# Two blocks of a small model on one core: the modulation vector computed beside three other stages, out of the first feed-forward

## What is computed

```python
c_act = jax.nn.silu(c)                       # c: (1, 1024)
ada = c_act @ w_ada[l] + b_ada[l]            # w_ada: (1024, 6144)
sh_m, sc_m, g_m, sh_f, sc_f, g_f = jnp.split(ada, 6, axis=-1)
h = modulate(rms_norm(x), sh_m, sc_m)        # h * (1 + scale) + shift
...                                          # second mixer: projections of h, rwkv and S5, w_out
x = x + g_m[:, None, :] * mix
h = modulate(rms_norm(x), sh_f, sc_f)
ffn = (jax.nn.silu(h @ ffn_w_gate[l]) * (h @ ffn_w_up[l])) @ ffn_w_down[l]
x = x + g_f[:, None, :] * ffn
```

## Time and profile before

| | us |
|---|---|
| median of 3 runs | 3499.85 |
| lowest and highest | 3493.99, 3503.96 |
| time of the profiled execution | 3495.26 |
| its span, first to last instruction | 3493.4 |
| PE busy | 3265.6 (93%) |
| DVE busy | 2001.5 (57%) |
| ACT busy | 1230.2 (35%) |
| POOL busy | 899.0 (26%) |
| granted clock of TensorE, mean | 0.957 of full |

### The profile page before, as it was taken

One profiled execution on the slowest core, in us unless ns is written; L12 is line 12 of the kernel. 1 busy time (PEld: TensorE's weight loads), 2 busy tenths in 40 slices (PEclk: granted clock), 3 DMA queues, 4 the chain that ended last, 5 costly groups with the idle time before them and its releaser, 6 DMA issues. The chain is left out here.

```text
span 3493.4 us, 56038 instructions
## 1 busy us (share of the span) xinstructions
PE 3265.6 (93%) x22553; PEld 2699.0 (77%) x22553; DVE 2001.5 (57%) x3144; ACT 1230.2 (35%) x2077; POOL 899.0 (26%) x502
## 2 busy tenths in 40 slices
PE   8999999999999989899899899979988979999999
PEld 7878888877887767777778777768776758888887
DVE  5852566533875567778778536144433355455685
ACT  3111222122665134344345421235332143333443
POOL 2332333346110432222200044132221332222000
PEclk9999999999999989999999999979998989999999
DMA  4454334334001423444374355220010313323742
GB/s 127 139 186 128 121 109 121 112 112 135 9 9 52 139 71 129 141 160 151 118 263 141 100 166 130 91 97 22 21 39 17 118 55 115 111 91 100 264 134 97
DMA packets 355294, 387.95 MB, mean 111 GB/s; under 512 B 27328, under 2 KB 258290, under 8 KB 353834
## 3 DMA queue, kind: packets, MB, share of 16 engines
q1 hardware_dynamic: 327518, 303.89, 28.2%
q10 hardware_dynamic: 26560, 78.27, 5.9%
q0 software_dynamic: 960, 2.21, 0.3%
HBM read 271.98 MB, written 112.33 MB: 110 GB/s over the span
## 5 line engine op out<-in xcount | busy, mean ns | idle before, releaser
L1104 PE MATMUL bk<-ffn_bhi,ffn_ahi 128*128 128x512 f32 x1240 | 492.2, 401 | 68.7 <-ACT ffn_u L1314 33.6
L1104 PE MATMUL bk<-ffn_blo,ffn_ahi 128*128 128x512 f32 x1240 | 487.8, 398 | 0.0
L1104 PE MATMUL bk<-ffn_bhi,ffn_alo 128*128 128x512 f32 x1240 | 486.9, 397 | 0.0
L1070 POOL TENSOR_TENSOR ffn_alo<-ffn_raw,ffn_ahi 128x512 fp32r<-128x512 f32 x134 | 222.8, 1673 | 722.1 <-ACT ffn_ahi L1245 722.1
L223 PE MATMUL acc<-h_hi,whi 128*128 128x512 f32 x1136 | 374.8, 409 | 23.2 <-DVE h_lo L2800 6.7
L223 PE MATMUL acc<-h_lo,whi 128*128 128x512 f32 x1136 | 358.1, 394 | 0.0
L223 PE MATMUL acc<-h_hi,wlo 128*128 128x512 f32 x1136 | 356.9, 393 | 0.0
L206 POOL TENSOR_TENSOR whi<-raw,ones 128x1024 fp32r<-128x1024 f32 (+1 forms) x83 | 155.9, 1879 | 755.7 <-PE acc L223 562.2
L1104 PEld LDWEIGHTS bk<-ffn_bhi,ffn_ahi 128*128 128x128 f32 x1240 | 238.9, 193 | 130.6 <-issue 77.0
L1104 PEld LDWEIGHTS bk<-ffn_bhi,ffn_alo 128*128 128x128 f32 x1240 | 239.1, 193 | 51.5
L1104 PEld LDWEIGHTS bk<-ffn_blo,ffn_ahi 128*128 128x128 f32 x1240 | 239.5, 193 | 49.9
(11 more groups left out here) (601 smaller groups left out, 6479.9 us busy)
## 6 DMA issues: line engine op xcount, KB each, us to landing
ffn_graw<-ffn_gated SPq DMA_DIRECT2D x154, 256.0 KB, 2.7
raw<-w_in SPq DMA_DIRECT2D x51, 512.0 KB, 4.0
projT<-proj_stage ACTq DMA_DIRECT2D x51, 512.0 KB, 3.1
ffn_ada_raw<-w_ada SPq DMA_DIRECT2D x12, 2048.0 KB, 8.9
ffn_raw<-w_up SPq DMA_DIRECT2D x44, 512.0 KB, 6.7
ffn_gated<-ffn_gout SPq DMA_DIRECT2D x44, 512.0 KB, 3.3
ffn_gated<-ffn_gt SPq DMA_DIRECT2D x22, 768.0 KB, 6.2
ffn_drow<-w_down SPq DMA_DIRECT2D x44, 256.0 KB, 6.0
```

Of the source, the lines that this page charges most:

```text
L1070: nc.gpsimd.tensor_tensor(a_lo[:, slot], source, a_hi[:, slot], ALU.subtract).then_inc(s[f"low{slot}"], 1)
L1104: ins = nc.tensor.matmul(o, wt[:, w, k, :], xt[:, x, k, :], start=first and i == 0, stop=last and i == 2, skip_group_check=reopened)
```

## The change

The modulation leaves the first feed-forward and becomes a class `Modulation`, used in three stages: 6 chunks beside the product with `w_out` in the first mixer output, 2 beside units 4 and 6 of the second projections, 4 beside units 2 to 5 of the second mixer output. The scaling on ACT and the tree on DVE become one chain on DVE: one `tensor_scalar` of 128x512 and seven `scalar_tensor_tensor` of 128x512, each of which waits for the one before it (`Steps.link`). The column sums stay on PE, the bias on DVE, which now adds the 1 of the scales too. A stage has one or two buffers of 2 MB for the matrix (`raw_at`); with `n` of them, load i waits on SP for the weighing of chunk i-n. `silu(c)` is computed in place by ACT at the start of the first mixer output. The second mixer's output is written out as a stage of its own, `second_mixer_out`, with the same order of work as `residual_gemm`.

```diff
@@ TwoNorms.programs
-            act.wait_ge(s["ada_ready"], 2)
...
-            for group in (1, 4):
-                c = prm[:, ADA + group * KD:ADA + (group + 1) * KD]
-                nc.vector.tensor_scalar(c, c, 1.0, None, ALU.add).then_inc(s["ada_ready"], 1)
@@
+class Modulation:
+    def load(self, sp, s, i):
+        n, c = len(self.raw), self.first + i
+        if i >= n:
+            sp.wait_ge(s["ada_part"], i - n + 1)
+        sp.dma_start(self.raw[i % n][:], self.w_ada[:, :, c * ADA_W:(c + 1) * ADA_W]).then_inc(s[f"ada_in{i % n}"], 16)
+
+    def weigh(self, dve, s, i):
...
+        dve.wait_ge(s[f"ada_in{i % n}"], 16 * (i // n + 1))
+        if i >= 2:
+            dve.wait_ge(s["ada_summed"], i - 1)
+        steps = Steps(dve, s["ada_step"], (KD - 1) * i)
+        steps.link(nc.vector.tensor_scalar(part[:], raw[:, 0, :], factor(0), None, ALU.mult))
+        for k in range(1, KD):
+            last = nc.vector.scalar_tensor_tensor(out=part[:], in0=raw[:, k, :], scalar=factor(k), in1=part[:], op0=ALU.mult, op1=ALU.add)
+            if k < KD - 1:
+                steps.link(last)
+        last.then_inc(s["ada_part"], 1)
+
+    def column_sums(self, pe, s, i, bank):
+        pe.wait_ge(s["ada_part"], i + 1)
+        if i > 0:
+            pe.wait_ge(s["ada_taken"], i)
+        for j in range(ADA_W // P):
+            last = self.nc.tensor.matmul(bank[:, j:j + 1], self.part[i % 2][:, j * P:(j + 1) * P], self.ones[:, 0:1], start=True, stop=True)
+        last.then_inc(s["ada_summed"], 1)
@@ attention_and_mixer_out: SP, PE, ACT, DVE
+                if u == KD + 1:
+                    sp.wait_ge(s["products_done1"], KD // 2)
+                if 0 <= u - KD - 1 < mod.count:
+                    mod.load(sp, s, u - KD - 1)
...
                 three_pass(nc, acc[b], w_hi[b], w_lo[b], x_hi, x_lo, n, ready=ready).then_inc(s[f"products_done{b}"], 1)
+                if 0 <= u - KD - 1 < mod.count:
+                    mod.column_sums(pe, s, u - KD - 1, ada)
...
+            c = prm[:, PRM["c_2"]:PRM["c_2"] + KD]
+            nc.scalar.activation(c, c, ACT.Silu).then_inc(s["c_done"], 1)
...
             for u in range(KD):
                 add(u)
                 add_square(u)
+                if 0 <= u - 2 < mod.count:
+                    mod.take(dve, s, u - 2, ada)
+                if u < mod.count:
+                    mod.weigh(dve, s, u)
@@ feed_forward: load_modulation, scale_modulation, weigh, column_sums, take and their calls go
@@ second_mixer_out (FIRST_CHUNK = 2): SP, PE, DVE
+                sp.dma_start(raw[b][:], weight(u)).then_inc(s[f"weight_loaded{b}"], 16)
+                if 0 <= u - FIRST_CHUNK - 1 < mod.count:
+                    mod.load(sp, s, u - FIRST_CHUNK - 1)
...
+                three_pass(nc, acc[b], w_hi[b], w_lo[b], hi, lo, KD, ready=ready).then_inc(s[f"products_done{b}"], 1)
+                if 0 <= u - FIRST_CHUNK - 1 < mod.count:
+                    mod.column_sums(pe, s, u - FIRST_CHUNK - 1, ada)
...
+                add(u)
+                add_square(u)
+                if 0 <= u - FIRST_CHUNK - 2 < mod.count:
+                    mod.take(dve, s, u - FIRST_CHUNK - 2, ada)
+                if 0 <= u - FIRST_CHUNK < mod.count:
+                    mod.weigh(dve, s, u - FIRST_CHUNK)
@@ projections2_and_s5: SP (behind the weights of unit u), PE, DVE (behind the read of unit u-1)
+                if u in (2, 4):
+                    mod.load(sp, s, u // 2 - 1)
...
                 if gh == 0:
+                    pe.wait_ge(s["ada_taken"], mod.count)
...
+                if u in (4, 6):
+                    mod.column_sums(pe, s, u // 2 - 2, tot[:, 0, :])
...
-            steps.do(nc.vector.memset(V[:, :, :, 0:1], 0.0))
...
+                if u in (5, 7):
+                    mod.take(dve, s, (u - 5) // 2, tot[:, 0, :])
+                if u in (4, 6):
+                    mod.weigh(dve, s, u // 2 - 2)
+                if u == Z_SLOT:
+                    dve.wait_ge(s["ada_summed"], mod.count)
+                    steps.do(nc.vector.memset(V[:, :, :, 0:1], 0.0))
@@ build: chunks (first, count) and the addresses in KB of the buffers for the matrix
+                            Modulation(nc, mem, env, "mix", w_ada, 0, 6, (40, 72), 100))
+    ... Modulation(nc, mem, env, "proj2", w_ada, 6, 2, (136,), 152) ...
+                     Modulation(nc, mem, env, "mix2", w_ada, 8, 4, (156, 172), 188))
```

More of the change, by code:

```diff
@@ L660, in _ @@
             sp.wait_ge(s["stored"], 16 * NT)
[L663 to L707, removed]
 def columns(w, k_tiles):
@@ L713, in columns, with __init__, take @@
     return lambda u: v[:, :, bass.ds(u * P, P)]
-def attention_and_mixer_out(nc, mem, env, projT, yaT, w_nsa, w_out, merged, sums, xmid):
-    xT, hi, lo = env["xT"], env["hi"], env["lo"]
+ADA_W = 4 * P
+class Modulation:
+    SEMS = "ada_in0 ada_in1 ada_step ada_part ada_summed ada_taken "
+    def __init__(self, nc, mem, env, name, w_ada, first, count, raw_at, part_at):
+        self.nc, self.prm, self.ones, self.w_ada, self.first, self.count = nc, env["prm"], env["ones"], w_ada, first, count
+        self.raw = [mem.at(f"{name}_ada_raw{i}", a, [P, KD, ADA_W]) for i, a in enumerate(raw_at)]
+        self.part = [mem.at(f"{name}_ada_part{i}", part_at + 2 * i, [P, ADA_W]) for i in range(2)]
+    def load(self, sp, s, i):
[4 more added lines that the diff above has]
+    def weigh(self, dve, s, i):
+        nc, n = self.nc, len(self.raw)
+        raw, part = self.raw[i % n], self.part[i % 2]
+        factor = lambda k: self.prm[:, PRM["c_2"] + k:PRM["c_2"] + k + 1]
+        dve.wait_ge(s[f"ada_in{i % n}"], 16 * (i // n + 1))
[15 more added lines that the diff above has]
+        last.then_inc(s["ada_summed"], 1)
+    def take(self, dve, s, i, bank):
+        n, c = ADA_W // P, self.first + i
+        out, bias = (self.prm[:, a + n * c:a + n * c + n] for a in (ADA, PRM["b_ada_2"]))
+        dve.wait_ge(s["ada_summed"], i + 1)
+        self.nc.vector.scalar_tensor_tensor(out=out, in0=bank[:, 0:n], scalar=1.0 if n * c // KD in (1, 4) else 0.0, in1=bias,
+                                            op0=ALU.add, op1=ALU.add).then_inc(s["ada_taken"], 1)
@@ L727, in attention_and_mixer_out @@
+def attention_and_mixer_out(nc, mem, env, projT, yaT, w_nsa, w_out, merged, sums, xmid, mod):
+    xT, prm, hi, lo = env["xT"], env["prm"], env["hi"], env["lo"]
     m_hi, m_lo = merged
@@ L738, in attention_and_mixer_out @@
     names = both("weight_loaded weight_high weight_split products_done acc_read other_in")
-    names += "gate_in0 gate_in1 gate_in2 gate_in3 gate_on summed high low square_done sum_done x_kept "
-    with phase(nc, mem, names, [(f"acc{b}", [P, NH, HALF], F32) for b in range(2)]) as (block, s, ps):
-        acc = [ps["acc0"], ps["acc1"]]
+    names += "gate_in0 gate_in1 gate_in2 gate_in3 gate_on summed high low square_done sum_done x_kept c_done " + mod.SEMS
+    banks = [(f"acc{b}", [P, NH, HALF], F32) for b in range(2)] + [("ada", [P, HALF], F32)]
+    with phase(nc, mem, names, banks) as (block, s, ps):
+        acc, ada = [ps["acc0"], ps["acc1"]], ps["ada"]
         def loads_of(u):
@@ L886, in half_rows, with feed_forward @@
     return order
-def feed_forward(nc, mem, env, name, up, down, kind, norm, sums, spill, xsave, gate=None, w_ada=None):
+def feed_forward(nc, mem, env, name, up, down, kind, norm, sums, spill, xsave, gate=None):
     xT, prm, ident, ones = env["xT"], env["prm"], env["ident"], env["ones"]
@@ L1176, in p3 @@
                 product(S4_B22, bank_c(p), False)
[L1178 to L1186, removed]
             def down_product(i, n):
@@ L1290, in high_s4 @@
                 high(S4_B22, s4[:], p + 1)
[L1292 to L1297, removed]
-                    nc.scalar.activation(ada_raw[:, k, :], ada_raw[:, k, :], ACT.Copy, scale=c_act[:, k:k + 1]).then_inc(s["ada_scaled"], 1)
             def high_t(slot, t, made):
@@ L1393, in _ @@
             high_t(A22_T4, T4, "t4_made")
-            if w_ada is not None:
-                nc.scalar.activation(c_act[:], prm[:, PRM["c_2"]:PRM["c_2"] + KD], ACT.Silu).then_inc(s["c_done"], 1)
             high_12(2)
@@ L1701, in _ @@
                     low_s3(p + 1)
-                if p in ada_chunks:
-                    weigh(ada_chunks[p])
             read_c12(LAST)
```

130 lines of the change are left out of this document (74 added, 56 removed).

## The result

| | before | changed |
|---|---|---|
| median of 6 runs, us | 3500.67 | 3520.91 |
| lowest and highest | 3493.99, 3506.26 | 3514.47, 3530.73 |
| ratio, 95% interval | | 1.0071 (1.0056 to 1.0085) |
| span of the profiled execution | 3493.4 | 3529.0 |
| PE busy | 3265.6 | 3279.5 |

The forecast was 3463, faster with a chance of 0.90. The change is slower by 20 us. The profiled execution of the changed kernel is its slowest (3530.73), that of the kernel before one of its shortest (3495.26), so the two profiles lie 35 us apart where the medians lie 20. So its stages are read one by one and its total is not used; to which stages the other 15 us belong, no trace shows.

A forecast was written before the change was run, and what follows sets the result against it. PE, busy 93% of the span, was taken as the bound. Terms -66.6 + 6.9 + 16.5 + 6 = -37.2 gave 3458 against the profiled execution, 3463 us with the median's 4.6; range 3447 to 3484.

The forecast's parts named there:

- The chain has a deadline, since PE makes chunk i's sums behind the next unit's products: First mixer output: PE waits 0.3 us for the first chunk's chain, 0.1 to 0.2 for each later one.
- The first feed-forward: Its up part loses waits on `copy_u2` and `copy_u3`, slow clock and column sums: -66.6 us.
- Its term for the clock: First feed-forward's up part: clock 0.97 against 1.00 over 446.2 us, worth 13.4 us.
- The chain: DVE's weighing of one chunk, one `tensor_scalar` and seven linked `scalar_tensor_tensor`: 6.0 us.
- the mixers' other terms: Column sums, chain waits and tail in the mixer outputs: +6.9 us in the first, +6 in the second.
- the half chance of POOL: Second mixer output: with half a chance, POOL once gets in before DVE's last link, 1.90 us more.
- The silu: Start of first mixer output: small activation and second table load end before the gate's landing; cost 0.
- The second projections: Unit 5's weights queue behind load 1, so PE idles, then half clock and sums: +16.5 us (13 to 21).
- the landing of the weights: Second projections: unit 5's weights land 8.5 to 9.5 us behind the large load's issue, later with other traffic.
- (a): Mixer outputs: POOL gets ahead of every chain's last link, 19 us, 25 with half clock: 3488; chance 0.11.
- (c): Second projections: stall lasts longer, units 6, 7 and S5's inputs late too, 26 for 16.5: 3473; chance 0.12.
- (d): First feed-forward's waits belong to convolution and GELU; only column sums come back, -10.8 against 29.4: 3518; chance 0.04.

The follow-up runs named there:

- experiment 8: Kernel before the change, once without two of the three tree additions: 3446.63 us; once without ACT's 96 scalings: 3476.91 us.
- the kernel of both: Changed kernel with two PSUM banks for the column sums and the second projections' second load moved behind unit 6's weights: 3445.70 us.
- experiments 3 and 4: Changed kernel with the second projections' second load behind unit 6's weights: 3513.39 us; the same with two PSUM banks for the column sums: 3445.70 us.

## Why the prediction was wrong

**The step that failed** is "The chain has a deadline, since PE makes chunk i's sums behind the next unit's products". It costed one of the two waits ahead of the sums, that for the chain, with care (0.3, then 0.1 to 0.2 each). The other, for the taking of the chunk before, appears in my text only as a small addition to the chain's length, "with the bias ahead of it 11.9". I asked how long the taking lasts and never where it stands. The earlier trace rows had the answer: the taking follows the addition that ends at 1191.22 + 2.83 = 1194.05, and PE reaches the sums just ahead of 1188.5, so 5.6 us of waiting for each chunk but the first of a stage. Eight times 5.6 is 45; measured 43.2 (the last of each stage waits 4.2, since no split runs beside it). With the 1.7 us of half clock that the text took for a short stall, the eight would have added 8 x 7.3 = 58 to -37: +21. That this is the distance of the medians, +20.2, is in part chance. By the stages of the two profiles the eight waits cost 43.2 + 26.4 = 69.6, with twice the clock of that sum, and the stages add up to +33.3. All the rest of the forecast, -37.2, came to 33.3 - 69.6 = -36.3, because its misses cancel: -0.6 in the feed-forward, -2.9 in the mixers, +4.4 in the projections.

**Point by point.** The first feed-forward: forecast -66.6, measured -67.2, waits on `copy_u2` gone, clock 1.00. The size is right; the cause is right but for the tree's own wait for ACT and for the sums, of which the text says nothing (experiment 8). Its term for the clock, 13.4, was 16.3 by PE's busy time (405.96 - 378.82 - 10.8), and leaves nothing for small gaps; the whole difference was taken, so the sum does not change. The chain: forecast 6.0, measured 0.47 + 7 x 0.75 + gaps, 1184.0 to 1190.0. The first chunk's wait: forecast 0.3, measured

```profile
1190.05 1.05 PE L708 MATMUL ada<-ones,mix_ada_part 128*128 128x1 f32 x8 [0.15 <-DVE mix_ada_part L698]
```

With the taking out of the way the mixers' other terms are 6.2 against 6.9, and 3.4 against 6 (4.7 in the kernel of both), at the foot of its range of 4.5 to 8 or under it, since the half chance of POOL did not come. The silu: table load, activation (0.21) and second table load stand back to back from 1113.54 to 1116.34, and ACT then idles 2.44 for the gate. The drain that the prediction's estimate put between them does not show, and no wait of PE came. The second projections: forecast +16.5 within 13 to 21, measured +20.9: 17.5 of wait in place of 12.5, 1.8 of sums, 1.6 of clock. The mechanism was right to each step, and the mis-sized term was the landing of the weights, 16.3 us behind their issue in place of 9, where the text allowed up to 12.6 behind the large load for other traffic. The earlier trace rows came from a stretch in which no other queue moved anything, and here 2.85 MB went beside.

**Rivals.** (a), POOL ahead of the last link, did not happen: 70 links of 0.750 to 0.754 in the mixers. (c), S5's inputs late as well and 26 in all, did not happen: the stall was longer than forecast, but PE did not wait for those inputs, which came into play only once the load was moved (experiments 3 and 4). (d) gave 3518, beside the 3520.9 measured, and is still wrong: it kept the feed-forward's waits, and those went. The right number there is chance. What was missing is a rival in which the new sums wait for something other than their input.

## What to carry to other kernels

A semaphore that guards the reuse of a small buffer is a wait like any other: price it by what stands ahead of the releasing instruction on its engine, not by that instruction's duration. If what stands ahead depends on the waiting engine's latest work, the wait is a round trip in each iteration, and either a second buffer or moving the release ahead of that work removes it. Write down each `wait_ge` that a change adds to the busiest engine with the time at which it is satisfied, and bound a transfer's landing by the traffic of the stage that it goes to.

## What was not expected of the hardware

- An idle PE costs twice. Eight waits of 4.2 to 6.0 us, 43.2 in all, brought 26.4 us of slower products. Eight waits of 1.5 us, 12.0 in all, brought 9.1, and there the clock fell behind three of them only.
- The link with one tensor in SBUF as its input is held up by POOL as well: `tensor_scalar` of 128x512 took 0.45 and 0.47 alone, and 2.41 beside POOL's low part, from 2090.60 to 2093.01, while POOL's ended at 2090.34 + 2.39 = 2092.73 (both in the timeline of the changed kernel, second projections). By the Trainium skill ("SBUF — State Buffer", "Who interferes with whom") `tensor_scalar` can take the shared ports too; the trace agrees.
- The rwkv stage, the same code in all, took 433.8 to 446.5 us between profiles. Where a stage has many short waits, one profile is no base for a few microseconds.
